# One encoder layer on one core: the modulation's block and the projection's block made one, and the waits for the projection's last stores moved into the attention's block

## The reference, cut to what matters

```python
mod = jnp.einsum('bd,de->be', jax.nn.silu(c), w_ada[l]) + b_ada[l]
sh1, sc1, g1, sh2, sc2, g2 = jnp.split(mod[:, None, :], N_MOD, axis=-1)
h = _layer_norm(x) * (1 + sc1) + sh1
proj = jnp.einsum('bsd,de->bse', h, w_in[l])
q, k, v, u = jnp.split(proj, [QK_WIDTH, 2 * QK_WIDTH, 2 * QK_WIDTH + ATTN_WIDTH], axis=-1)
q = _apply_rope(q.reshape(b, s, N_ATTN_HEADS, 2, QK_DIM), cos, sin)
k = _apply_rope(k.reshape(b, s, N_ATTN_HEADS, 2, QK_DIM), cos, sin)
```

## Time and profile before

| | |
|---|---|
| median of 3 runs | 3055.91 us (3055.81 to 3057.52) |
| the profiled execution | 3050.71 us |
| its span, first to last instruction | 3048.9 us |
| mean granted TensorE clock | 0.982 |
| busy share: TensorE, VectorE, ScalarE, GpSimd | 95%, 70%, 42%, 46% |
| modulation's block | 0 to 54.4 us |
| projection's block | 55.1 to some 510.4 us |
| attention's first instruction | 511.68 us |

### The profile page before, as it was taken

How to read it: one execution, slowest core, us unless ns; L and a number is a source line. 1 busy time by engine, 2 the same in 40 slices (tenths; PEclk the granted TensorE clock), 3 DMA queues, 4 the chain that set the end, 5 groups by cost and what they waited for, 6 DMA issues and landing times.

```text
span 3048.9 us, 39408 instructions
## 1 busy us (share of the span) xinstructions
PE 2902.0 (95%) x14244; PEld 2437.1 (80%) x14244; DVE 2139.3 (70%) x3093; ACT 1276.7 (42%) x2286; POOL 1409.1 (46%) x1110
## 2 busy tenths in 40 slices
PE   7999998899999998999689999999999999999996
PEld 3888886666666656888679999989999989999995
DVE  5666654988888865566566666677778666777767
ACT  2111112777777764456543233343333333333334
POOL 0233321011111125568745455475677566666655
PEclk9999999999999998999899999999999999999998
DMA  7333346221312105466431221242322224323322
GB/s 246 125 124 126 126 142 168 51 70 56 82 56 70 50 28 200 130 211 206 158 128 56 83 70 57 96 169 70 125 91 96 90 92 148 107 95 104 109 68 94
DMA packets 194061, 333.02 MB, mean 109 GB/s; under 512 B 15366, under 2 KB 102599, under 8 KB 193866
## 3 DMA queue, kind: packets, MB, share of 16 engines
q1 hardware_dynamic: 193868, 330.49, 33.5%
HBM read 250.72 MB, written 79.71 MB: 108 GB/s over the span
## 4 chain that ended last, share of the span: by engine, by line
PE 51%; POOL 3%; DVE 3%; issue 1%; DVEq 1%; POOLq 1%; ACT 1%; DMA 1%; SPq 0%; ACTq 0%
PE tail_bank L2306 9%; PE tail_bank L2308 9%; PE tail_bank L2307 9%; PE tail_bank L2330 5%; PE tail_bank L2331 5%; PE tail_bank L2332 5%; POOL tail_rounded L2042 1%; PE tail_bank L2245 1%; PE tail_bank L2243 1%; PE tail_bank L2244 1%; POOL tail_rounded L2050 1%; PE tail_bank L2192 0%; PE tail_bank L2184 0%; PE tail_bank L2185 0%; POOL tail_rounded L2055 0%
## 5 line engine op out<-in xcount | busy, mean ns | idle before, releaser
L2042 POOL TENSOR_TENSOR tail_rounded<-tail_plain,tail_rounded 128x512 fp32r<-128x512 f32 x462 | 649.2, 1426 | 490.8 <-ACT tail_rounded L1827 490.5
L2306 PE MATMUL tail_bank<-tail_rounded 128*128 128x384 f32 x1848 | 622.0, 337 | 35.4 <-ACT tail_plain L1847 10.4
L2307 PE MATMUL tail_bank<-tail_rounded 128*128 128x384 f32 x1848 | 620.4, 336 | 0.0
L2308 PE MATMUL tail_bank<-tail_rounded 128*128 128x384 f32 x1848 | 620.3, 336 | 0.0
L2466 DVE TENSOR_TENSOR tail_plain<-tail_plain,tail_bank 128x384 f32<-128x384 f32 x462 | 247.9, 549 | 283.8 <-PE tail_bank L2308 211.3
L1827 ACT ACTIVATE tail_rounded<-tail_plain 128x512 fp32r<-128x512 f32 x462 | 271.5, 621 | 377.3 <-DVE tail_plain L2444 184.3
L2306 PEld LDWEIGHTS tail_bank<-tail_rounded 128*128 128x128 f32 x1848 | 349.1, 189 | 39.8 <-issue 34.4
L2307 PEld LDWEIGHTS tail_bank<-tail_rounded 128*128 128x128 f32 x1848 | 349.2, 189 | 1.3
L2308 PEld LDWEIGHTS tail_bank<-tail_rounded 128*128 128x128 f32 x1848 | 349.0, 189 | 0.0
L1165 DVE TENSOR_REDUCE att_peak<-att_sc 128x1 f32<-128x1024 f32 x256 | 312.8, 1222 | 45.3 <-PE att_sc L978 38.5
L2330 PE MATMUL tail_bank<-tail_rounded 128*128 128x512 f32 x792 | 309.5, 391 | 16.1 <-issue 7.1
(11 more groups left out here) (286 smaller groups left out, 5144.0 us busy)
## 6 DMA issues: line engine op xcount, KB each, us to landing
tail_plain<-in_w_gu SPq DMA_DIRECT2D x132, 512.0 KB, 4.8
keep_ahead<-in_w_dn SPq DMA_DIRECT2D x66, 512.0 KB, 6.6
proj_ada<-in_w_ada SPq DMA_DIRECT2D x16, 1024.0 KB, 5.9
held_w_hi<-scr_qs_d SPq DMA_DIRECT2D x128, 128.0 KB, 2.8
scr_h_d<-tail_plain SPq DMA_DIRECT2D x63, 256.0 KB, 4.5
tail_plain<-scr_h_d SPq DMA_DIRECT2D x45, 256.0 KB, 4.3
w_in_x_in<-in_x SPq DMA_DIRECT2D x18, 512.0 KB, 6.4
scr_att_d<-held_w_hi SPq DMA_DIRECT2D x36, 256.0 KB, 2.9
```

Source lines behind the costliest of these rows:

```text
L2042: nc.gpsimd.tensor_tensor(w_lo[:, j, :], operand(F, j), w_hi[:, j, :].bitcast(F32), ALU.subtract).then_inc(wlo_done, 1)
L2306: nc.tensor.matmul(dst, w_hi[:, j, cols], h_hi[j][:, k, :], start=(k == 0), stop=False)
L2307: nc.tensor.matmul(dst, w_hi[:, j, cols], h_lo[j][:, k, :], start=False, stop=False)
L2308: m = nc.tensor.matmul(dst, w_lo[:, j, cols], h_hi[j][:, k, :], start=False, stop=(k == 3))
```

## The change

- `modulation` is gone. Its instructions stand at the head of `project`'s streams, in one block and one scope. Its tiles lie in tiles of the projection not yet in use (`wa` in `ada`, `turned` and `u`; the sums in `acc`; the columns in `qk_tp`). One barrier and one clearing of semaphores between the two are gone, and only one scope is cleared after the projection.
- VectorE splits pieces 0 to 2 between `norm(0)` and `norm(1)`.
- The first `h_hi` and `h_lo` are made in two halves with semaphores of their own (`h_half`, `hhi_half`, `hlo_half`). TensorE starts tile 0 on the first half and transposes tile 1 after tile 0's first chunk, not ahead of tile 0.
- ScalarE splits 10 pieces ahead of `h_hi` (12 before); both engines split pieces up to 17 ahead of tile 1's modulate (15 and then 19 before).
- The load of x tile 2 is issued after piece 24 (ahead of the projection's pieces before). The first `ada` load also waits for the last `wa` use.
- The copies of bias and lambda by VectorE come after piece 31 (after piece 15 before).
- The gate rows are stored ahead of the last `up_d` store. The six store semaphores live in the outer scope, SP doesn't wait for them at the projection's end, and the attention waits for them: SP after its first query loads, VectorE ahead of everything.

The diff, cut to its core:

```diff
-def modulation(nc, keep, first, x, rope, cT, w_ada, b_ada, lam_in, w_in, w_hi, w_lo):
+def project(nc, keep, x, cT, w_ada, b_ada, lam_in, mod_rows, w_in, w_hi, rope, qs_d, ks_d, v_d, up_d, fold_d, b0_d, mid_d, q_landed, k_first, stored):
...
+        wa = [tile[:].rearrange(form).rearrange("p (h c) -> p h c", h=2) for tile, form in (
+            (ada, "p k c -> p (k c)"), (turned, "p a b c -> p (a b c)"), (u, "p k c -> p (k c)"))]
...
+            for n in range(pieces, PIECES):
+                piece(n)
+                if n == 3 * KD:
+                    load_x(2)
             load_ada(0)
...
+                if t == NT - 1:
+                    store_gates()
                 if t >= ST:
                     sp.wait_ge(u_done, t + 1)
                     sp.dma_start(up_d[t - ST], u[:, t - ST, :]).then_inc(up_stored, 16)
-            sp.wait_ge(gates_out, 1)
...
-            sp.wait_ge(gates_stored, 64)
-            sp.wait_ge(mid_stored, 16)
-            sp.wait_ge(up_stored, 16 * PT)
-            sp.wait_ge(v_stored, 16 * NT)
-            sp.wait_ge(qk_stored, 64 * NT)
-            sp.wait_ge(fold_stored, folds(ST // 4))
...
+            for n in range(10):
+                split_w(n)
+            act.wait_ge(h_half, 1)
+            nc.scalar.activation(h_hi[:, 0, 0:KD // 2, :], h_raw[:, 0:KD // 2, :], ACT.Copy).then_inc(hhi_half, 1)
+            act.wait_ge(h_done, 1)
+            nc.scalar.activation(h_hi[:, 0, KD // 2:, :], h_raw[:, KD // 2:, :], ACT.Copy).then_inc(hhi_done, 1)
+            for n in range(10, SPLIT_AHEAD):
                 split_w(n)
...
+            pool.wait_ge(hhi_half, 1)
+            nc.gpsimd.tensor_tensor(h_lo[:, 0, 0:KD // 2, :], h_raw[:, 0:KD // 2, :], h_hi[:, 0, 0:KD // 2, :].bitcast(F32),
+                                    ALU.subtract).then_inc(hlo_half, 1)
...
+            pe.wait_ge(hlo_half, 1)
             for t in range(NT):
-                if t + 1 < NT:
+                if 0 < t < NT - 1:
                     transposes(t + 1)
...
                         m = products(c, k, t % 2)
                     m.then_inc(chunk_done[c], 1)
+                    if c == 0 and t == 0:
+                        transposes(1)
...
+            norm(0)
+            for n in range(3):
+                split_w(n)
+            norm(1)
+            for n in range(3, 10):
+                split_w(n)
+            add_bias()
+            take_cols()
+            modulate(0)
+            for n in range(10, SPLIT_AHEAD):
                 split_w(n)
...
+        def projection_stored(eng):
+
+            qk_stored, v_stored, up_stored, fold_stored, mid_stored, gates_stored = left
+            eng.wait_ge(qk_stored, 64 * NT)
+            eng.wait_ge(v_stored, 16 * NT)
+            eng.wait_ge(up_stored, 16 * PT)
+            eng.wait_ge(fold_stored, 16 * (ST + 1))
+            eng.wait_ge(mid_stored, 16)
+            eng.wait_ge(gates_stored, 64)
...
             load_q(1)
+            projection_stored(sp)
             load_v(0)
...
         def _(dve):
+            projection_stored(dve)
             nc.vector.memset(halves[:], -0.5)
```

## The result

| | before | after |
|---|---|---|
| median of 12 runs each | 3052.64 us (3049.54 to 3057.52) | 3057.51 us (3052.16 to 3064.19) |
| the profiled execution, its span | 3050.71, 3048.9 | 3064.19, 3062.4 |

What follows compares the result with a forecast made beforehand. TensorE was taken to bound the projection, 440.6 of 443.8 us busy. T0 1.2, pieces -0.9 and the projection's end 4.8 gave 5.1 us won, from 3055.91 to 3050.8, range 3046 to 3054.5.

Steps and rivals of the forecast that it cites:

- Everything later should shift as a whole: Stages behind the two places, projection start and end, were to move in time without gaining or losing: 0 us.
- All later tiles have VectorE ahead of need: In projection tiles after tile 1's start, TensorE was not to wait for VectorE: no loss forecast.
- fourth rival: Also the slower rival: clock low through the whole first tile, 0.46 us per low microsecond, 4.0 us slower, 3059.9; chance 0.04.
- Place (b): Projection's end, from TensorE's last product to the attention's first score: 4.8 us won, between 3.9 and 4.9.
- Place (a): Projection's start, before TensorE's steady pace: tile 1 starts at +37.3 instead of +36.4, 0.9 us lost relative to T0.
- T0: Start of the first modulate, 44.90 us before; +x means T0 + x us; forecast 1.2 us earlier, between 0 and 2.0.
- the term of 0: Second half of modulate(0) beside a GpSimd operation: not slowed, 0 us; 1.2 us if blocked.
- rival 2: Clock falls while TensorE waits for pieces; part of tile 1 at half speed, 1 to 2 us, 3052.3; chance 0.20.
- rival 3: At the projection's end the store wait only changes its place, (b) worth nothing, 3055.6; chance 0.06.
- The early start: Rival 1: first products move from about 57.0 to 47.1 and count in full, 14.7 us won, 3041.2; chance 0.12.

Runs made afterwards that it cites:

- after_again: The changed kernel unaltered, run and profiled a second time: 3056.53 us, ratio to the kernel before 1.0020.
- after_aligned: The changed kernel with 320 unused bytes per partition ahead of its first projection tile, so tiles start at multiples of 512 bytes: 3052.64 us, ratio to before 0.9994.
- before_shifted: The kernel before with 192 unused bytes per partition ahead of `u`, no instruction altered: 3063.38 us, ratio to before 1.0028.
- b_only: The kernel before with only the waits for the projection's last stores moved into the attention; gate rows still last: 3051.37 us, ratio to before 1.0002.
- a_only: The changed kernel with store waits and gate-row stores back at the projection's end, none in the attention: 3059.87 us, ratio to before 1.0029.
- ada_early_before: The kernel before with each modulation load issued once VectorE has summed the one before, ahead of the stores: 3050.48 us, ratio to before 0.9987.
- ada_early_after: The changed kernel with each modulation load issued once VectorE has summed the one before, ahead of the stores: 3045.98 us, ratio to before 0.9980.

## Why the prediction was wrong, by its own steps

- **"Everything later should shift as a whole" and "All later tiles have VectorE ahead of need"** is the step that failed, and it failed by more than all the others. My first row showed 440.6 of 443.8 us busy, and the missing 3.2 us were exactly TensorE waiting for VectorE, in three tiles. There was no reserve, and the diff touched the chain behind those waits: stores, then the modulation load in SP's queue, its landing, 5.9 us of sums, a modulate of 2.6 us, the sums over partitions. I read the tiles' new order in SBUF as bookkeeping. It cost 0.26% (`after_again` against `after_aligned`) or 0.28% (`before_shifted`), some 8 us: longer waits (3.2 to 8.2) and more time at the low clock. The tiles 6, 10 and 14 take longer than the tiles of the same form beside them, by 5.5 us in sum before, by 16.7 in `after_again` and by 14.4 in `before_shifted`. For the 8.2 us that `after_again` lost in this stretch the sum is, as an estimate: 5.0 of waits; 6.3 of clock (the mean granted clock from 85 to 495 us is 0.979 against 0.996, which is some 13.6 us more at the low level, at the 0.46 each of my fourth rival); less 3.0 for products that ran closer together (see the last section).
- **Place (b), 4.8 us.** The mechanism was right in the main: TensorE's gap shrank, and VectorE waited for the `up_d` store. The size was not. `b_only` brings its first maximum 2.6 us closer to the last product, the ten profiles with the waits moved 3.4 us on average (13.4 to 10.0). The terms that were off are SP's: I had kept 1.34 us for the last head store and 1.36 for the gate rows, and they took 2.21 and 2.87. The first goes with the tiles' place: 0.86 to 1.91 us in the nine profiles with the heads at an offset of 0 or 256, 2.04 to 2.36 in the five with them at 192. The second goes with the order: in `a_only`, which issues the gate rows last, they took 1.34 and the `up_d` store 1.83, where after has 2.87 and 0.35, and both end 4.3 us after the last product's start. So storing the gate rows first won nothing. The first score came 1.37 us after SP's last issue, where I had 0.98. The last receipt, which I had put 5.6 us behind the last product's start (509.5, from a share of 0.05 at 509), came 7.1 behind it; the bytes were the same, their time was not. It didn't set the first maximum, as the row at 517.87 shows.
- **What (b) wins is partly given back.** From the first maximum to the last ring product four kernels with the old waits took 638.1 to 639.2 us, the ten profiles with the new ones 638.4 to 641.3, 1.4 us more on average. `b_only` is 3.35 us ahead of before at the first maximum and 0.16 at the ring; 1.5 us of that go in a few steps over the 132 maxima, the other 1.7 behind the last one. Its cause I did not find. In the tail the four kernels with the old waits took 1893.6 to 1893.9 us, the ten profiles with the new ones 1890.6 to 1901.0, 3.0 more on average; with one profile of each it isn't shown that the waits do it. The whole time of `b_only` shows no gain: its interval is -1.8 to +3.4 us, which excludes 4.8.
- **Place (a).** Piece 31 at +35.3 (forecast +34.9), first product +3.4 as worked out, tile 1 at +37.7 (+37.3). Over all profiles the one-block kernels start tile 1 at +38.3 on average, the others at +36.4: 1.9 us lost, not 0.9. T0 came 1.7 us earlier on average (43.6 against 45.4) where I had 1.2. The two cancel: tile 1 starts at 81.9 and at 81.8.
- **The modulate beside GpSimd** took 2.64 us as before, though GpSimd's subtraction on the first half ran beside its last 0.5 us (from 46.61), so the term of 0 was right; the sentence of the Trainium skill, "SBUF — State Buffer", section "Who interferes with whom", agrees with it.
- **The rivals.** The clock did fall in the waits for pieces (in after the mean of 70 to 77 us is 0.52). In eight of the ten one-block profiles that cost nothing, because tile 0 was waiting for VectorE anyway: tile 1 starts 2.4 us behind piece 31, at the clock of 1.00. In `after_again` it starts 3.5 us behind it and in `after_aligned` 4.7, since tile 0's last products ran at the low level (0.50 from 78 to 82 us in `after_aligned`). So rival 2's mechanism is real and cost 1 to 2 us in two profiles of ten, in tile 0 and not in tile 1. Its sign, a low clock after 80, came mainly from the later waits, and rival 3's, a first maximum later than 513, came from the late last product. The early start did not count in full. My slower rival was a clock that stays low in tile 0, which did not happen. None of the rivals was about the projection's steady part, where the time went.

What is left of the change when the heads are put back at an aligned place is -0.9 us over four kernels (0.9994, 0.9985, 1.0003, 1.0006). The profiles would give more: +0.1 at tile 1, -1.3 from there to the last product (these four kernels against before), and -2.0 at the end after what is given back. What takes the rest is open; the tail was 4.6 us longer in these four profiles than in that of before. With the early loads the change is worth more: 0.9962 against 0.9987.

## What to carry to other kernels

- A stage that is 99% busy is not free of waits: find which make the missing 1%, and follow every instruction and transfer of the chain behind them through the diff.
- When a change adds, drops or reorders tiles, compare the addresses of what the small-row DMAs read. Two kernels that differ in nothing but 192 bytes differed by 8.6 us.
- A load that everyone waits for belongs in the queue as early as its buffer allows, not behind stores. That one move took all three waits away and won some 10 us in the changed kernel, 4 in the kernel before.

## What the runs showed of the hardware that I had not expected

- SP's time to issue one DMA is no fixed price: the last head store, 0.57 us at tile 10 before, took 0.86 to 2.36 us over the fourteen profiles at the projection's end, behind eight key loads of 256 KB, and the gate rows 1.35 or 2.5 to 2.9 by their place in the queue.
- A wait of 0.5 to 1.3 us ahead of the sixteen tiny products of `add_partitions` (1.92 us) was followed by a low clock in some profiles and not in others; with no wait there it never was.
- The one-block kernels multiply slightly faster. Between the transposes of two tiles without sums lie 23.74 us in the two-block kernels and 23.55 to 23.58 in the others, spread evenly over the 96 products (0.229 us from one to the next against 0.227), whatever the pad. From tile 1 to the last product it comes to 3.0 us: 417.1 in `ada_early_before` against 414.1 to 414.2 in the three one-block kernels with early loads. Its cause is not settled. The rows are of `ada_early_before` and of `ada_early_after`:

```profile
279.13 1.04 PE L549 MATMUL w_in_tp<-keep_ident,w_in_x_in 128*128 128x128 f32 x8
302.87 1.03 PE L549 MATMUL w_in_tp<-keep_ident,w_in_x_in 128*128 128x128 f32 x8
```

```profile
276.11 1.03 PE L433 MATMUL proj_tp<-keep_ident,proj_x_in 128*128 128x128 f32 x8
299.67 1.03 PE L433 MATMUL proj_tp<-keep_ident,proj_x_in 128*128 128x128 f32 x8
```
